# Three waits in a float32 hybrid block: filter-tap buffers, the last two input tiles, and the second half's sums of squares

## What is computed

```python
h  = rmsnorm(x, g_mix_pre) * (1 + sc_m) + sh_m        # the shifts, scales and gates come from c and ada_w
hc = rmsnorm(ctx, g_mix_pre) * (1 + csc_m) + csh_m
p, pc = h @ w_in, hc @ w_in                           # 1024 x 2816
y = concat([hyena(p, filters), neighbourhood_attention(p, pc), rglru(p, pc)]) @ w_out
x = x + gt_m * rmsnorm(y, g_mix_post)
h = rmsnorm(x, g_ffn_pre) * (1 + sc_f) + sh_f
g, u = split(h @ w_gu)                                # 2 x 2816
x = x + gt_f * rmsnorm((silu(g) * u) @ w_down, g_ffn_post)
```

## Time and profile before

| | us |
|---|---|
| median of 3 runs | 1537.72 (1537.6 to 1542.82) |
| the profiled execution, its own time | 1543.49 |
| its span, from the first to the last instruction | 1541.7 |
| mean granted TensorE clock, as a share of full speed | 0.964 |
| TensorE busy | 1429.8 |

### The profile page before, as it was taken

How to read it: one execution, slowest core, us unless ns; L and a number is a source line. 1 busy time by engine, 2 the same in 40 slices (tenths; PEclk the granted TensorE clock), 3 DMA queues, 4 the chain that set the end, 5 groups by cost and what they waited for, 6 DMA issues and landing times.

```text
span 1541.7 us, 20500 instructions
## 1 busy us (share of the span) xinstructions
PE 1429.8 (93%) x7699; PEld 1163.0 (75%) x7699; DVE 743.7 (48%) x1036; ACT 540.9 (35%) x845; POOL 617.3 (40%) x285
## 2 busy tenths in 40 slices
PE   4899999989998999899899999999998999999994
PEld 1388677879986777678677888878877888877883
DVE  5563647892845778537874111133356111111235
ACT  3662553312314667634332222232222222321220
...
GB/s 322 257 179 75 42 28 31 134 37 113 50 33 97 122 117 118 136 110 84 135 69 82 95 95 95 96 88 99 99 82 113 119 95 98 93 104 77 102 85 54
DMA packets 236697, 156.54 MB, mean 102 GB/s; under 512 B 11043, under 2 KB 222385, under 8 KB 236507
## 3 DMA queue, kind: packets, MB, share of 16 engines
...
## 4 chain that ended last, share of the span: by engine, by line
PE 78%; DVE 12%; ACT 3%; POOL 3%; issue 2%; DMA 1%; SPq 1%; ACTq 0%; DVEq 0%
PE ps L1786 32%; PE ps L1791 16%; PE ps L1944 10%; PE ps L1947 5%; PE ps L2100 2%; POOL w_lo L1071 1%; PE ps L2066 1%; PE ps L2077 1%; DVE a_f L1640 1%; PE ps L1960 1%; DVE a_f L1678 1%; PE ps L1835 1%; DVE pr L1622 1%; DVE x L1679 1%; PE ps L1841 1%
## 5 line engine op out<-in xcount | busy, mean ns | idle before, releaser
L1055 POOL TENSOR_TENSOR w_lo<-raw,w_hi 128x1024 fp32r<-128x1024 f32 x152 | 371.6, 2445 | 466.5 <-ACT w_hi L668 466.5
L1786 PE MATMUL ps<-hb_hi,w_hi 128*128 128x512 f32 x832 | 328.9, 395 | 22.8 <-DVE g_t L1707 12.2
L1786 PE MATMUL ps<-hb_lo,w_hi 128*128 128x512 f32 x832 | 327.0, 393 | 0.0
L668 ACT ACTIVATE w_hi<-raw 128x1024 fp32r<-128x1024 f32 x152 | 160.0, 1053 | 186.8 <-PE ps L1791 179.4
L1791 PE MATMUL ps<-hb_hi,w_lo 128*128 128x512 f32 x832 | 207.9, 392 | 1.9 <-POOL w_lo L1055 1.9
L1786 PEld LDWEIGHTS ps<-hb_hi,w_hi 128*128 128x128 f32 x832 | 158.2, 190 | 59.6 <-DVE g_t L1707 13.3
L1071 POOL TENSOR_TENSOR w_lo<-raw,w_hi 128x1024 fp32r<-128x1024 f32 x22 | 96.1, 4369 | 232.3 <-ACT w_hi L823 232.3
L1791 PEld LDWEIGHTS ps<-hb_hi,w_lo 128*128 128x128 f32 x832 | 156.6, 188 | 36.7 <-POOL w_lo L1055 2.3
L1786 PEld LDWEIGHTS ps<-hb_lo,w_hi 128*128 128x128 f32 x832 | 158.3, 190 | 32.5
L1944 PE MATMUL ps<-ha_hi,w_hi 128*128 128x512 f32 (+2 forms) x432 | 164.7, 381 | 3.7 <-ACT w_hi L823 3.3
L1944 PE MATMUL ps<-ha_lo,w_hi 128*128 128x512 f32 (+2 forms) x432 | 162.0, 375 | 0.0
...
## 6 DMA issues: line engine op xcount, KB each, us to landing
raw<-in_ffn_w_gu SPq DMA_DIRECT2D x88, 512.0 KB, 3.8
ada1x<-in_ada_w SPq DMA_DIRECT2D x32, 512.0 KB, 4.0
raw<-in_ffn_w_down SPq DMA_DIRECT2D x32, 512.0 KB, 4.0
raw<-in_w_in SPq DMA_DIRECT2D x22, 512.0 KB, 4.0
ada<-in_ada_w SPq DMA_DIRECT2D x4, 2048.0 KB, 22.8
raw<-in_w_out SPq DMA_DIRECT2D x16, 512.0 KB, 4.0
...
raw<-in_ktab SPq DMA_DIRECT2D x8, 512.0 KB, 7.2
```

The source lines that it names most:

```text
L668: act.activation(w_hi[:, b, :], raw[:, b, :], ACT.Copy).then_inc(hi_done, 1)
L1055: pool.tensor_tensor(w_lo[:, b, :], raw[:, b, :], w_hi[:, b, :].bitcast(F32), ALU.subtract).then_inc(lo_done, 1)
L1786: pe.matmul(dst, w_hi[:, b, k * P:(k + 1) * P], x, start=start and k == 0 and n == 0, stop=False)
```

## The change

It has four parts. (1) The three rows of `rowsC` are loaded by SyncE's queue, ahead of everything else there; TensorE makes the first layer before it turns `rowsC`; the semaphores are regrouped. (2) `kabs` gets two buffers and `kmax` three, `filter_norm` is moved one pair of taps later in TensorE's program, three of the eight tap rests (`DVE_SPLIT`) go from GpSimd to VectorE, GpSimd's first table rest comes one tap later, and VectorE's preparation of `silp` goes ahead of the loop. (3) Input tiles 8 and 9 get buffers of their own and are loaded earlier in SyncE's program. (4) In the first half's feed-forward the squares are taken in two groups of four around `gu_tile(0)`, the sum over the features and `rstd_of(2)` come one tile later, the eight `add_mixed` are spread as 1, 2, 2, 2, 1 over tiles 1 to 5 instead of 3, 3, 2, `x_turns` follows them, and tiles 4 to 6 are written out ahead of the loop. The residual input of the second half (`xr2`) has a buffer of its own too. The lines that only rename semaphores, index the new buffers or move the loops' first tile from 4 to 7 are left out.

```diff
+DVE_SPLIT = (1, 3, 5)
...
-kmax = at("kmax", H_ + 22528, [2, 2 * HY])
-kabs = at("kabs", H_, [2, 2 * HY])
+kmax = [at(f"kmax{r}", a, [2 * HY]) for r, a in enumerate((H_ + 22528, H_ + 24576, H_ + 8192))]
+kabs = [at("kabs0", H_, [2, 2 * HY]), at("kabs1", H_ + 4096, [2, 2 * HY])]
...
+late_tiles = [at("late0", H_ + 30720, [2, ALL]), at("late1", H_ + 71680, [2, ALL])]
+def xin_all(n):
+    return late_tiles[n - 8][:, :, 6 * P:10 * P] if n >= 8 else xin[n % 6][:].rearrange("p (a c) -> p a c", a=2)
+def xin_cols(n, k):
+    return xin_all(n)[:, k // 4, (k % 4) * P:(k % 4 + 1) * P]
...
+    sp.dma_start(rowsC[0:1, :].rearrange("p (a n) -> p a n", a=2), A["hy_f_b1"].unsqueeze(1).broadcast_to([1, 2, 64])).then_inc(id_ld, 16)
...
+    sp.dma_start(rowsC[2:4, :].rearrange("p (a n) -> p a n", a=2), A["hy_f_freq"][0].unsqueeze(1).broadcast_to([2, 2, 64])).then_inc(id_ld, 16)
...
-    sp.dma_start(hrow[0:1, :], A["hy_bias"].rearrange("a o c -> a (o c)")).then_inc(hrow_ld, 16)
+    sp.dma_start(hrow[0:1, :], A["hy_bias"].rearrange("a o c -> a (o c)")).then_inc(par_ld, 16)
...
-        sp.dma_start(xin[n % 6][:], src[t * P:(t + 1) * P, :]).then_inc(x_ld[n % 6], 16)
+        landed = late_ld[n - 8] if n >= 8 else x_ld[n % 6]
+        sp.dma_start(xin_all(n), src[t * P:(t + 1) * P, :].rearrange("p (a c) -> p a c", a=2)).then_inc(landed, 16)
...
+    sp.wait_ge(ada_mm, 4)
+    x_dma(8)
...
+    sp.wait_ge(x_sq, 10)
+    x_dma(9)
...
-    sp.wait_ge(x_tp, 2 * KT)
-    x_dma(8)
-    x_dma(9)
...
-    act.dma_start(rowsC[0:1, :].rearrange("p (a n) -> p a n", a=2), A["hy_f_b1"].unsqueeze(1).broadcast_to([1, 2, 64])).then_inc(flt_ld, 16)
...
-    act.dma_start(rowsC[2:4, :].rearrange("p (a n) -> p a n", a=2), A["hy_f_freq"][0].unsqueeze(1).broadcast_to([2, 2, 64])).then_inc(flt_ld, 16)
...
-        act.dma_start(w12[64 * j:64 * j + 64, 1, :], A["hy_f_w2"][0]).then_inc(flt_ld, 16)
+        act.dma_start(w12[64 * j:64 * j + 64, 1, :], A["hy_f_w2"][0]).then_inc(id_ld, 16)
...
-            act.wait_ge(k_max, t)
...
-        act.activation(kabs[:], eo[:, TILE[t]], ACT.Abs).then_inc(k_abs, 1)
+        if t >= 2:
+            act.wait_ge(k_max, t - 1)
+        act.activation(kabs[t % 2][:], eo[:, TILE[t]], ACT.Abs).then_inc(k_abs, 1)
...
-        act.wait_ge(x_ld[n % 6], 16 * (n // 6 + 1))
-        act.activation(xin[n % 6][:], xin[n % 6][:], ACT.Copy, scale=rx[:, n:n + 1]).then_inc(x_n, 1)
+        if n >= 8:
+            act.wait_ge(late_ld[n - 8], 16)
+        else:
+            act.wait_ge(x_ld[n % 6], 16 * (n // 6 + 1))
+        act.activation(xin_all(n), xin_all(n), ACT.Copy, scale=rx[:, n:n + 1]).then_inc(x_n, 1)
...
-        for i in range(4):
-            gu_tile(i, (lambda: root(2)) if (h, i) == (0, 1) else (lambda: root(4)) if (h, i) == (1, 0) else None)
-        with act.Fori(4, FT) as i:
+        i0 = 4 if h else 7
+        for i in range(i0):
+            gu_tile(i, (lambda: root(2)) if (h, i) == (0, 2) else (lambda: root(4)) if (h, i) == (1, 0) else None)
+        with act.Fori(i0, FT) as i:
...
-        pool.wait_ge(e_hi, n + 1)
-        pool.tensor_tensor(eo_lo[:, k].rearrange("p x c -> p (x c)"), eo[:, k].rearrange("p x c -> p (x c)"),
-                           eo_hi[:, k].bitcast(F32).rearrange("p x c -> p (x c)"), ALU.subtract).then_inc(e_lo, 1)
-        if n in (2, 6):
-            k_rest(n // 4)
+        if n not in DVE_SPLIT:
+            pool.wait_ge(e_hi, n + 1)
+            pool.tensor_tensor(eo_lo[:, k].rearrange("p x c -> p (x c)"), eo[:, k].rearrange("p x c -> p (x c)"),
+                               eo_hi[:, k].bitcast(F32).rearrange("p x c -> p (x c)"), ALU.subtract).then_inc(e_lo, 1)
+        if n in (3, 6):
+            k_rest(n // 6)
...
-        if t >= 2:
-            dve.wait_ge(k_acc, t - 1)
-        dve.tensor_tensor(kmax[:, t % 2], kabs[:, 0], kabs[:, 1], ALU.max).then_inc(k_max, 1)
+        if t >= 3:
+            dve.wait_ge(k_acc, t - 2)
+        dve.tensor_tensor(kmax[t % 3][:], kabs[t % 2][:, 0], kabs[t % 2][:, 1], ALU.max).then_inc(k_max, 1)
+    def tap_rest(n):
+        k = SPLIT[n]
+        dve.wait_ge(e_hi, n + 1)
+        dve.tensor_tensor(eo_lo[:, k].rearrange("p x c -> p (x c)"), eo[:, k].rearrange("p x c -> p (x c)"),
+                          eo_hi[:, k].bitcast(F32).rearrange("p x c -> p (x c)"), ALU.subtract).then_inc(e_lod, 1)
...
+    dve.wait_ge(silt_ok, 1)
+    dve.wait_ge(silp_ok, 1)
+    link(dve.scalar_tensor_tensor(sil_t[:], sil_t[:], 1.0, colA[:, 0:16], ALU.add, ALU.mult))
+    link(dve.tensor_scalar(sil[:].rearrange("p a b -> p (a b)"), sil_t[:], 0.5, None, ALU.mult))
+    dve.tensor_copy(silp[:, :, 0:2], sil[:].rearrange("p a k -> p k a")).then_inc(sil_ok, 1)
...
-        if p == 1:
-            dve.wait_ge(silt_ok, 1)
-            dve.wait_ge(silp_ok, 1)
-            link(dve.scalar_tensor_tensor(sil_t[:], sil_t[:], 1.0, colA[:, 0:16], ALU.add, ALU.mult))
-            link(dve.tensor_scalar(sil[:].rearrange("p a b -> p (a b)"), sil_t[:], 0.5, None, ALU.mult))
-            dve.tensor_copy(silp[:, :, 0:2], sil[:].rearrange("p a k -> p k a")).then_inc(sil_ok, 1)
+        if p >= 2:
+            tap_rest(2 * p - 3)
...
+    tap_rest(5)
...
-    dve.wait_ge(hrow_ld, 16)
+    dve.wait_ge(par_ld, 16 * 17)
...
-            for k in range(KT):
-                dve.wait_ge(acc_free, E_OUT + KT + k + 3)
-                add_square(yo[1][:, k, :], k, nrm, a_f)
+            def mixed_squares(ks):
+                for k in ks:
+                    dve.wait_ge(acc_free, E_OUT + KT + k + 3)
+                    link(dve.tensor_tensor(nrm[:] if k == 0 else sq[:, 1, :], yo[1][:, k, :], yo[1][:, k, :], ALU.mult))
+                    if k:
+                        link(dve.tensor_tensor(nrm[:], nrm[:], sq[:, 1, :], ALU.add))
+            mixed_squares(range(0, 4))
+            gu_tile(0)
+            mixed_squares(range(4, 8))
...
-            gu_tile(0)
+            gu_tile(1)
...
-            gu_tile(1)
-            add_mixed(1, range(0, 3))
-            gu_tile(2)
-            add_mixed(1, range(3, 6))
-            gu_tile(3)
-            add_mixed(1, range(6, 8))
+            add_mixed(1, range(0, 1))
+            for i, ks in ((2, range(1, 3)), (3, range(3, 5)), (4, range(5, 7)), (5, range(7, 8))):
+                gu_tile(i)
+                add_mixed(1, ks)
...
+            gu_tile(6)
...
-    pe.wait_ge(id_ld, 16)
-    pe.wait_ge(flt_ld, 112)
-    pe.transpose(ps[:, 6, 142:146], rowsC[0:4, :], ident[0:4, 0:4]).then_inc(colc_ps, 1)
+    pe.wait_ge(flt_ld, 32)
...
+    pe.wait_ge(id_ld, 96)
+    pe.transpose(ps[:, 6, 142:146], rowsC[0:4, :], ident[0:4, 0:4]).then_inc(colc_ps, 1)
...
-    pe.wait_ge(par_ld, 16 * 16)
+    pe.wait_ge(par_ld, 16 * 17)
...
-                    pe.wait_ge(e_lo, i + 1)
+                    if i in DVE_SPLIT:
+                        pe.wait_ge(e_lod, DVE_SPLIT.index(i) + 1)
+                    else:
+                        pe.wait_ge(e_lo, i + 1 - sum(d < i for d in DVE_SPLIT))
...
-        if p:
-            filter_norm(2 * p - 2)
-            filter_norm(2 * p - 1)
-    filter_norm(RAD - 2)
-    filter_norm(RAD - 1)
+        if p >= 2:
+            filter_norm(2 * p - 4)
+            filter_norm(2 * p - 3)
+    for t in range(RAD - 4, RAD):
+        filter_norm(t)
...
-            gu_tile(1, lambda: sum_over_features(2, nrm))
-            gu_tile(2)
-            x_turns(range(12, 15))
+            gu_tile(1)
+            gu_tile(2, lambda: sum_over_features(2, nrm))
...
+            x_turns(range(12, 13))
+            gu_tile(4)
+            x_turns(range(13, 15))
+            gu_tile(5)
...
+            gu_tile(6)
```

More of the change, by code:

```diff
@@ L248, in program @@
         yo = [at("yo0", P_KV, [KT, HALF]), at("yo1", P_KV + 16384, [KT, HALF])]
-        xr2 = at("xr2", P_HY + 8192, [4, D])
+        xr2 = [at("xr2", P_HY + 8192, [4, D]), at("xr3", P_HY + 24576, [4, D])]
         yd = at("yd", S_ + 32768, [KT, HALF])
@@ L314, in program @@
         lfree = [sem("lfree0"), sem("lfree1")]
-        lhi, llo, ljob, x_r, k_bias, hrow_ld, v_ed = [sem(n) for n in ("lhi", "llo", "ljob", "x_r", "k_bias", "hrow_ld", "v_ed")]
+        lhi, llo, ljob, x_r, k_bias, e_lod, v_ed = [sem(n) for n in ("lhi", "llo", "ljob", "x_r", "k_bias", "e_lod", "v_ed")]
         kraw_ld = [sem("kraw_ld0"), sem("kraw_ld1")]
@@ L344, in program @@
                              "n_tp", "n_x1", "n_h", "n_hh", "n_hl", "bst_ok", "f_mm")]
-        g_tanh, g_a, g_ah, g_al, dn_done, dn_free, y_ok = [
-            sem(n) for n in ("g_tanh", "g_a", "g_ah", "g_al", "dn_done", "dn_free", "y_ok")]
+        g_tanh, g_a, g_ah, g_al, dn_free = [
+            sem(n) for n in ("g_tanh", "g_a", "g_ah", "g_al", "dn_free")]
+        late_ld = [sem("late_ld0"), sem("late_ld1")]
         o_tp, o_ev, st_out = sem("o_tp"), sem("o_ev"), [sem("st_out0"), sem("st_out1")]
@@ L434, in _ @@
         def _(sp):
+            sp.dma_start(rowsC[0:1, :].rearrange("p (a n) -> p a n", a=2), A["hy_f_b1"].unsqueeze(1).broadcast_to([1, 2, 64])).then_inc(id_ld, 16)
```

(21 more changed lines are left out.)

1 line of the change is left out of this document (removed).

## The result

The changed kernel takes **1517.87 us** (median of 4 runs, 1515.61 to 1520.78) against 1540.0 for the kernel before in the same comparison (4 runs, 1537.6 to 1542.82): a ratio of 0.9857, 95% interval 0.9828 to 0.9885, or 22.1 us. The forecast was 1514.2 in a range of 1509 to 1524. The profiled execution took 1515.61 us with a span of 1513.8, 27.9 less than the one of before. TensorE is busy for 1418.0 us (94%), and its mean granted clock is 0.974, where it was 0.964.

A forecast was written before the change was run, and what follows sets the result against it. TensorE, busy for nearly the whole span, bounds the kernel, with waits where other engines stand in its chain. 4.1 + 4.2 + 5.6 + 9.6 = 23.5 takes 1543.49 to 1520.0; the median lies 5.8 lower, 1514.2, range 1509 to 1524.

The forecast's parts named there:

- Part 1: At the start, the earlier loads let the taps gain 4.1 us; ends 2.3 and 4.3.
- Part 2: In the taps, `spectrum(0)` ends 4.2 us sooner, t = 34.5 from the mended tap at 0; bounds 0, 6.
- Rival A: In the taps, three rests on VectorE each wait a whole GpSimd operation, 4.2 us lost: 1518.4; chance 0.15.
- Rival B: Up to the turns, loads set the pace; the start gains 4.0 us instead of 8.3: 1518.5; chance 0.12.
- Part 3: At the last input tiles' turns, a shorter wait and full clock save 5.6 us; 2.6 if the clock falls.
- Part 4: In the feed-forward's first tiles, idle time and slow clock fall from 13.6 to 4.0 us; gain 9.6.
- (a): Squares and sums behind `gu_tile(0)`, in tile 1's first product: L1707 ends 1.3 us after TensorE wants bank 0.
- (b): From the end of the feature sum, VectorE needs 9.6 us, TensorE allows 7.25: TensorE waits 2.4.
- (c): In tiles with two `add_mixed`, VectorE needs 10.7 us, TensorE 10.88; 0.3 us of waiting left.
- Rival C: In the feed-forward's first tiles, waits only move, through tile 5, and the clock falls: gain 3, 1520.8; chance 0.15.
- D: In the taps, the new buffers free nothing and the loop stays at 27.5 us: 1520.4; chance 0.05.
- E: In the feed-forward, short waits in tiles 2 to 5 keep the clock at 1.2 GHz: slower, 1546.9; chance 0.03.

The follow-up runs named there:

- e1_loads: The kernel before with only the first of the four parts, the reordered loads: 1532.45 us, ratio 0.9957.
- e2_taps: The kernel before with only the second part, the taps' buffers, order and three rests on VectorE: 1534.15 us, ratio 0.9978.
- e7_short_rests: The changed kernel with GpSimd's gate and up weight rests cut to 128 of 1024 columns in the first half's tiles 0 to 6: 1510.97 us, one run.
- e8_two_each: The changed kernel with the eight `add_mixed` spread as 2, 2, 2, 2 over tiles 2 to 5: 1520.47 us, ratio 0.9877.
- e9_silp_back: The changed kernel with VectorE's three `silp` operations back inside the loop, behind the second maximum: 1521.03 us, one run.
- e4_sums: The kernel before with only the fourth part, the second half's sums in the feed-forward: 1533.9 us, ratio 0.996.
- e6_one_kabs: The changed kernel with a single `kabs` buffer again, `kmax` keeping three: 1515.88 us, one run.
- e5_pool_rests: The changed kernel with all eight tap rests on GpSimd again, everything else kept: 1527.22 us, one run.

## Why the prediction was right, point by point

**Part 1, 4.1: mis-sized, 3.1.** The step that failed is the landing of `dec`: "lands near 11 and the second layer sets the pace". The second layer did end at 12.0, as forecast, but `dec` landed at 11.9, 7.4 us behind its issue, and VectorE could only then make `w3eo` and the argument that the second layer's sine needs. The value lies between the ends of 2.3 and 4.3, and `e1_loads` shows the same 3.06.

**Part 2, 4.2: mis-sized, 6.9 at the end of `spectrum(0)`.** The walk to the last `filter_norm` held: it ended at 46.98, t = 22.7, against a forecast of 22.8, and the waits behind GpSimd were four and made 6.2 us, where the walk had four and 6. But the bias step met less of GpSimd than I had counted: it ended at 50.25, t = 25.9, not 29.6. And I then followed the tap at 0 to the end of `spectrum(0)`, where TensorE itself sets it: `mod_sums` and 24 matmuls follow the last `filter_norm` without a gap and end at 56.2. With `mod_sums` at full clock, 3.64 for 5.61, that is 9.2 us where it was 11.3. So `spectrum(0)` gained 9.9 us and not 8.3, of which 3.05 are part 1's; the second `mod_sums` fell from 5.34 to 3.64 too, and with it the gain was 11.5. That gain of the clock, 3.7 us, was in no term of the sum. The first `mod_sums` takes 3.64 us in every trace with the whole of part 2, and 4.6 to 5.6 in the four without it. The 1.7 us of the second are luck: it takes 5.3 us in `e2_taps`, `e7_short_rests`, `e8_two_each` and `e9_silp_back`, and 3.64 in `e4_sums`, where the taps are as before.

What makes the loop shorter was also only partly as I said. I laid it to `Abs`, which "now waits for nothing but its window". Its second buffer is worth 0.4 us (`e6_one_kabs`), and the place of `silp` nothing (`e9_silp_back`). Of the 3.6 to 4.0 us by which VectorE's last maximum came earlier, the rests on VectorE bring 1.3 (`e5_pool_rests`). The other 2.4 to 2.7 come from what `e5_pool_rests` kept: the buffers, `filter_norm` one pair later, and GpSimd's table rest one tap later. The traces point to `filter_norm`: the two waits of VectorE's windows for TensorE's taps, 1.25 and 2.30 us before, are gone in every kernel that has it later. It was not moved alone, so this is argued and not shown.

Rival A, the port, is refuted for this kernel. One rest of three did wait, for 2.2 us (3.38 less 1.2), but moving them gained time, because they take turns with fewer operations of GpSimd. The Trainium skill's page "SBUF — State Buffer" (section "SBUF: two separate sides") calls the shared port pair "an exclusive lock"; the lengths of 1.65 and 7.18 / 3 us for a maximum of 0.68 in `e5_pool_rests` agree with it. What doesn't follow from it is that moving work between the two gains nothing: the same subtraction takes 1.2 us on VectorE and 2.4 on GpSimd, and moving three gained 1.3 us.

**Rival B, the loads.** Half of it came: ScalarE waits 3.5 us for the third table and 3.5 for the fourth, and the chain runs through them. But the fourth landed at 71.95, not at 75.8: where the prediction said that "the landings gain about 2 us", they gained 3.9; it was issued 2.5 us earlier and then took 11.6 us instead of 13.0, and why wasn't tried. The wait cost TensorE 0.21 us. By this trace the cover is used up, and more gained in the taps would be lost there; no run tried it.

**Part 3, 5.6: right against this trace of before.** 5.8 alone, 5.9 by the comparison, and 3.2 to 5.6 when every trace with the old buffers is set against every one with the new. In the whole change the wait was 1.90, 0.4 more than forecast; ScalarE finished its heads 0.3 us ahead of TensorE, where it had been 0.8 ahead. The clock stayed up behind it, as a wait of that kind had let it.

**Part 4, 9.6: nearly right alone, 2.0 short in the whole change.** Alone it made 9.3 (`e4_sums`), in the whole change 7.6 and in its repetition 8.0. (a) was forecast at 1.3, is 1.50 alone and 0.54 in the changed kernel, where tile 0 ran slower; (b) at 2.4 and is 2.19, ahead of tile 3, where it was put; (c) at 0.3 and is 0.23. The term that failed is the clock, which was in the lower bound and not in the sum: behind (b) sixteen matmuls last 5.5 us in the changed kernel, in its repetition, in `e5_pool_rests`, `e6_one_kabs` and `e9_silp_back` (3.63 at full clock), which costs 1.9. In `e4_sums` the same wait had no such group behind it. Rival C, waits that only move, is refuted: no wait in tiles 4 to 6 is over 0.3 us.

**Rivals D and E.** The whole of D, a loop that stays at 27.5, is refuted, although the buffer of `kabs` alone behaves nearly as D says. E never showed: no tile ran at 1.2 GHz through.

**The sum.** 23.5 forecast, 22.1 measured by the medians; the forecast of 1514.2 is 3.7 too low, 2.3 of it because the median of the kernel before is now 1540.0 and was 1537.7. By the two profiles the gain up to the input projection is 16.2, where parts 1 to 3 made 13.9 (part 1 gave 1.0 less, the clock in the two `mod_sums` 3.7 more); the feed-forward's first tiles gave 7.6 of 9.6, and behind them 0.5 is lost. That is 23.3. The other 4.6 of the 27.9 lie in the unchanged middle, and the medians don't show them. That the total comes so near is partly luck: parts 1 and 4 were taken 1 and 2 us too high, and a gain of the clock that nobody had forecast made up for them.
